# Expert weights in two steps of 1792 columns on one core of a Trainium2

## What is computed

```python
logits = (t @ router).astype(jnp.float32)
top_v, top_i = lax.top_k(logits, TOP_K)                  # TOP_K = 2 of 8
w = jax.nn.softmax(top_v, axis=-1)
combine = jnp.sum(jax.nn.one_hot(top_i, N_EXPERTS) * w[..., None], axis=1)
for e in range(N_EXPERTS):
    out = out + combine[:, e:e + 1] * swiglu(t, w_gate[e], w_up[e], w_down[e])
# swiglu(h, g, u, d) = (silu(h @ g) * (h @ u)) @ d;  g, u: 1024 x 3584, d: 3584 x 1024
```

## Time and profile before

| | us |
|---|---|
| median of 3 runs (1370.97 to 1372.62) | 1371.16 |
| span of the profiled execution, first to last instruction | 1370.1 |
| PE busy | 1328.3 (97%) |
| DVE busy | 735.9 (54%) |
| ACT busy | 630.0 (46%) |
| HBM read | 432.69 MB, 317 GB/s over the span |

### The profile page before, as it was taken

One profiled execution on the slowest core, in us unless ns is written; L12 is line 12 of the kernel. 1 busy time (PEld: TensorE's weight loads), 2 busy tenths in 40 slices (PEclk: granted clock), 3 DMA queues, 4 the chain that ended last, 5 costly groups with the idle time before them and its releaser, 6 DMA issues.

```text
span 1370.1 us, 16033 instructions
## 1 busy us (share of the span) xinstructions
PE 1328.3 (97%) x6410; PEld 936.1 (68%) x6410; DVE 735.9 (54%) x628; ACT 630.0 (46%) x573; POOL 29.0 (2%) x34
## 2 busy tenths in 40 slices
PE   7999999999999999999999999999999999999998
PEld 7978888888888875655665565665665656665665
DVE  6975444445653475454455455454645455455455
ACT  5855334444445463443453434444344444353442
POOL 2000000000310000000000000000000000000000
PEclk9999999999999999999999999999999999999999
DMA  9456556554542349999999999999999999999995
GB/s 333 164 184 216 188 192 193 193 186 128 181 153 92 132 165 361 413 414 414 400 415 409 399 413 413 408 410 409 404 408 412 406 412 410 410 404 413 411 402 225
DMA packets 127881, 434.79 MB, mean 317 GB/s; under 512 B 6960, under 2 KB 9120, under 8 KB 113472
## 3 DMA queue, kind: packets, MB, share of 16 engines
q1 hardware_dynamic: 127344, 433.11, 82.7%
q0 software_dynamic: 368, 0.63, 0.2%
q10 hardware_dynamic: 96, 0.03, 0.0%
HBM read 432.69 MB, written 1.05 MB: 317 GB/s over the span
## 4 chain that ended last, share of the span: by engine, by line
PE 74%; DMA 14%; ACT 4%; DVE 4%; issue 3%; SPq 1%; DVEq 0%; POOL 0%; POOLq 0%; ACTq 0%
PE ps L1381 16%; PE ps L1367 9%; PE ps L909 8%; PE ps L911 8%; PE ps L910 8%; PE ps L1368 8%; PE ps L1369 8%; DMA ring<-in_moe_w_gate_dram 8%; DMA ring<-in_moe_w_up_dram 4%; DVE lows L1533 2%; DMA ring<-in_moe_w_down_dram 2%; ACT whi L548 2%; PE ps L1312 1%; PE ps L1139 1%; SPq L455 1%
## 5 line engine op out<-in xcount | busy, mean ns | idle before, releaser
L1533 DVE TENSOR_TENSOR lows<-ring,whi 128x2048 fp32r<-128x2048 f32 x168 | 382.8, 2290 | 248.1 <-ACT whi L548 248.0
L548 ACT ACTIVATE whi<-ring 128x2048 fp32r<-128x2048 f32 x168 | 320.0, 1912 | 319.3 <-DMA ring<-in_moe_w_up_dram 113.6
L1381 PE MATMUL ps<-ring,xl 128*64 128x512 f32 (+1 forms) x1024 | 204.1, 544 | 4.9 <-DVE xl L2020 3.3
L1526 DVE TENSOR_TENSOR wlo<-raw,whi 128x2048 fp32r<-128x2048 f32 x73 | 166.5, 2288 | 73.5 <-PE ps L911 71.4
L1367 PE MATMUL ps<-whi,hT_hi 128*128 128x512 f32 x448 | 181.2, 405 | 13.0 <-DVE lows L1533 12.8
L541 ACT ACTIVATE whi<-raw 128x2048 fp32r<-128x2048 f32 x73 | 139.5, 1917 | 84.5 <-PE ps L911 82.9
L1368 PE MATMUL ps<-lows,hT_hi 128*128 128x512 f32 x448 | 175.0, 391 | 0.0
L1369 PE MATMUL ps<-whi,hT_lo 128*128 128x512 f32 x448 | 174.5, 390 | 0.0
L909 PE MATMUL ps<-whi,hT_hi 128*128 128x512 f32 x384 | 153.3, 399 | 2.4 <-DVE wlo L1526 1.4
L911 PE MATMUL ps<-whi,hT_lo 128*128 128x512 f32 x384 | 149.7, 390 | 0.0
L910 PE MATMUL ps<-wlo,hT_hi 128*128 128x512 f32 x384 | 149.5, 389 | 0.0
(11 more groups left out here) (307 smaller groups left out, 1314.6 us busy)
## 6 DMA issues: line engine op xcount, KB each, us to landing
ring<-in_moe_w_gate_dram SPq DMA_DIRECT2D x112, 1024.0 KB, 11.9
ring<-in_moe_w_up_dram SPq DMA_DIRECT2D x112, 1024.0 KB, 13.1
ring<-in_moe_w_down_dram SPq DMA_DIRECT2D x112, 1024.0 KB, 13.8
raw<-in_fox_w_in_dram SPq DMA_DIRECT2D x16, 1024.0 KB, 5.3
raw<-in_ffn_w_gate_dram SPq DMA_DIRECT2D x14, 1024.0 KB, 5.1
raw<-in_ffn_w_up_dram SPq DMA_DIRECT2D x14, 1024.0 KB, 5.1
raw<-in_ffn_w_down_dram SPq DMA_DIRECT2D x14, 1024.0 KB, 5.1
raw<-in_lru_w_in_dram SPq DMA_DIRECT2D x8, 1024.0 KB, 11.6
```

Of the source, the lines that this page charges most:

```text
L548: nc.scalar.activation(whi[:, 1 + q % SPLIT], ring[:, slot(i)], ACT.Copy).then_inc(hi_done, 1)
L1381: ins = mm(ps[g * HD:(g + 1) * HD, bank, 0:half], src(k), ring[:, slot(i), cols], start=first and k == 0, stop=last and k == tiles - 1, sk ...
L1526: nc.vector.tensor_tensor(wlo[:, m % LR], raw[:, m % RR], whi[:, m % HR].bitcast(F32), ALU.subtract).then_inc(lo_done, 1)
L1533: nc.vector.tensor_tensor(lows[:, slot(i)], ring[:, slot(i)], whi[:, 1 + q % SPLIT].bitcast(F32), ALU.subtract).then_inc(lo_done, 1)
```

## The change

The class `Group`, the two tables and the code of all five engines that handles the experts are rewritten; the two layers before them stay.

- The 3584 columns are cut in two steps of `W` = 1792. A gate or up unit is one row tile of 1792 columns, 0.9 MB, one run of 7 KB in each partition; a step has 8 of gate, 8 of up and 7 of down for each expert, and a pair has 92 units instead of 84. Names: G0, U0, D0 are the first step's stages, G1, U1, D1 the second's.
- A heavy gate or up unit is 12 matmuls of 448 columns over four banks (4 to 7), and gate, up and the heavy y (banks 4 and 5) use the same banks one after the other. A light unit is 4 calls of 448 columns; the two halves of the array take the even and the odd columns, so that they are read at a step of two.
- y leaves PSUM at the end of each step: `first_y` (ACT) writes the weighted sums of D0 to `yh` and `yl`, `second_y` (DVE) adds those of D1. They are fp32, and so is `ST`; the scatter is one fp32 matmul where it was two fp32r ones.
- D1 of a pair stands behind G0 of the next. A pair's order is G0, D1 of the pair before, U0, G1, D0, U1. After the last pair D1 stands alone (`TAIL`).
- Gathers come in four parts of 8 matmuls, and transposes of the heavy activations in parts of 8 and 6.

```diff
-PAIRS = 4
-PAIR_W = [2 * CW, 2 * CW, 2 * CW, CW]
-PAIR_U = [w // CW * 2 for w in PAIR_W]
+W = F // 2
+CB = W // 4
+TALL, DEEP = KT, W // (2 * P)
+RING, SPLIT = 10, 3
+SKIPS = (6, 25, 36, 47, 58, 69, 80, 90)
+
+
+def wide_turns(kind):
+
+    for b in range(0, TALL, 2):
+        for job in (0, 1):
+            for n in (b, b + 1):
+                yield job, kind, n
+
+
+def down_turns(kind):
+
+    for job, n in ((0, 0), (0, 1), (1, 0), (0, 2), (0, 3), (1, 1), (0, 4), (0, 5), (1, 2), (1, 3), (0, 6), (1, 4),
+                   (1, 5), (1, 6)):
+        yield job, kind, n
...
+REST = [*wide_turns("G1"), *down_turns("D0"), *wide_turns("U1")]
+TAIL = [*down_turns("D1")]
+BODY = [*wide_turns("G0"), *TAIL, *wide_turns("U0"), *REST]
...
+                    src = (moe_w_gate if kind[0] == "G" else moe_w_up)[0][expert, n * P:(n + 1) * P, col:col + W]
+                    sp.dma_start(ring[:, slot(pos), 0:W], src.rearrange("o p c -> p (o c)")
+                                 ).then_inc(arrived[slot(pos)], 16)
...
             pair_loads(Group(loops, 2))
+            pair_loads(Group(loops, 3, TAIL))
...
+            def first_y(group, job):
+
+                if job == 0 and group is not OPENING:
+                    act.wait_ge(m_scat[0], group.nth(0))
+                    act.wait_ge(m_scat[1], group.nth(0))
+                act.wait_ge(used, group.done(job, "D0"))
+                src, dst = (flat(HB, D), yh[:]) if job == 0 else (ps[:, LB], yl[:])
+                nc.scalar.activation(dst, src, ACT.Copy, scale=weight[:, job:job + 1]).then_inc(m_yw, 1)
...
-                for q, y in enumerate((y_hi[job], y_lo[job])):
-                    ins = mm(ps[:, bank], ST[rows, job, t * P:(t + 1) * P], y[rows, cols], start=job == 0 and q == 0,
-                             stop=job == 1 and q == 1)
-                return ins
+                return mm(ps[:, bank], ST[rows, job, t * P:(t + 1) * P], (yh, yl)[job][rows, cols], start=job == 0,
+                          stop=job == 1)
...
+            def wide_unit(group, job, kind, n):
+
+                pos = group.place[job, kind, n]
+                first, last = n == 0, n == TALL - 1
+                if job == 0:
+                    w_hi, w_lo = heavy_halves(group, pos)
+                    for b in range(4):
+                        dst, cols = ps[:, HB + b, 0:CB], slice(b * CB, (b + 1) * CB)
+                        mm(dst, xg_hi[:, n], w_hi[:, cols], start=first, stop=False)
+                        mm(dst, xg_hi[:, n], w_lo[:, cols], start=False, stop=False)
+                        ins = mm(dst, xg_lo[:, n], w_hi[:, cols], start=False, stop=last)
+                else:
+                    pe.wait_ge(arrived[slot(pos)], group.landed(pos))
+                    columns = ring[:, slot(pos), 0:W].rearrange("p (c g) -> p g c", g=2)
+                    for b in range(2):
+                        for g in range(2):
+                            ins = mm(ps[g * HD:(g + 1) * HD, LB + b, 0:CB], xl[:, n],
+                                     columns[:, g, b * CB:(b + 1) * CB], start=first, stop=last, skip_group_check=True)
                 ins.then_inc(used, 1)
...
+                for job, kind, n in wide_turns("U0"):
+                    if n == 0:
+                        pe.wait_ge(m_yd, prev.nth(1 + job, 2))
+                    wide_unit(group, job, kind, n)
+                    if (job, n) == (0, 3):
+                        pe.wait_ge(m_ST, prev.nth(1))
+                        scatter(0)
+                    if (job, n) == (0, 5):
+                        pe.wait_ge(m_acc, prev.nth(1, 2))
+                        scatter(1)
+                    if (job, n) == (0, 7):
+                        pe.wait_ge(m_acc, prev.nth(2, 2))
+                        pe.wait_ge(m_S, group.nth(1))
+                        pe.wait_ge(m_col, group.nth(1))
+                        selection_transposes(group)
...
+            nxt[0] = 0
+            lo_to(0, tail)
+            product(last, 1)
+            lo_to(1, tail)
+            act_T_lo(last, 1, 0)
+            act_T_lo(last, 1, 1, HB + 2)
+            light_product(last, 1)
+            lo_to(DEEP - 1, tail)
```

More of the change, by code:

```diff
@@ L180, in freed, with landed, split, done @@
-def freed(group, q):
-    return (HEAVY[q - SPLIT] - PAIR_UNITS if q < SPLIT else group.heavy[q - SPLIT]) + 1
+    def landed(self, pos):
+        s = slot(pos)
+        return at(16 * (LANDED[pos] - UNLED[s] + self.ahead * PER_SLOT[s]), 16 * PER_SLOT[s], self.i)
+    def split(self, q):
+        return at(N_MOE - HEAVY_LEAD + self.ahead * HEAVY_UNITS + q, HEAVY_UNITS, self.i)
+    def done(self, job, kind):
+        return self.units(max(pos for (j, k, _), pos in self.place.items() if (j, k) == (job, kind)) + 1)
@@ L185, in last_dense, with freed @@
+    def freed(self, q):
+        if self.table is OPEN and q < HEAVY_LEAD + SPLIT:
+            return N_MOE
+        p = max(p for p in range(q - 2 * SPLIT, q) if half_place(p) == half_place(q))
+        return self.units((self.heavy[p] if p in self.heavy else HEAVY_BODY[p + HEAVY_UNITS] - PAIR_UNITS) + 1)
 def last_dense(place):
@@ new lines, in pair_loads @@
+            def pair_loads(group):
+                experts = {}
+                if group is OPENING:
+                    experts["0", 0] = slice(FIRST, FIRST + 1)
+                for pos, (job, kind, n) in enumerate(group.table, group.first):
+                    if group is OPENING and pos in AHEAD:
+                        continue
+                    whose = "D1" if kind == "D1" else "0"
+                    if (whose, job) not in experts:
+                        experts[whose, job] = expert_of(group.before() if kind == "D1" else group, job)
+                    if group is not OPENING or last_in_slot(pos) >= LEAD:
+                        sp.wait_ge(used, group.units(last_in_slot(pos) + 1))
+                    load(group, pos, experts[whose, job])
@@ L817, in light_silu, with rows_view @@
[L817 to L824 removed]
+            def rows_view(bank, ks):
+                return ps[:, bank:bank + ks // 2].rearrange("p b n -> p (b n)").rearrange("p (k c) -> p k c", c=2 * P)
@@ L1372, in light_unit @@
-            def light_unit(group, i, src, bank, first, last):
-                width = group.table[i][4]
-                tiles = UK * CW // width
-                half = width // 2
-                pe.wait_ge(arrived[slot(i)], group.landed(i))
-                for k in range(tiles):
-                    for g in range(2):
-                        cols = slice(k * width + g * half, k * width + (g + 1) * half)
-                        ins = mm(ps[g * HD:(g + 1) * HD, bank, 0:half], src(k), ring[:, slot(i), cols],
-                                 start=first and k == 0, stop=last and k == tiles - 1, skip_group_check=True)
-                ins.then_inc(used, 1)
```

786 lines of the change are left out of this document (408 added, 378 removed).

## The result

The changed kernel takes **1389.3 us**, the kernel before 1371.9 in the same comparison: a ratio of 1.0117, 95% interval [1.0099, 1.0134]. The forecast was 1371, the range ended at 1387, so the kernel is slower by 18 us than forecast and lies outside. The profiled execution spans 1388.2 us.

A forecast was written before the change was run, and what follows sets the result against it. The bound was to move from DMA to PE: 210.3 + 0.6 + 0.7 + 2.6 = 214.2 us a pair against the stream's 211.3. Waits removed would pay for added work: 1371 us (own range 1366 to 1376), full range 1361 to 1387.

The forecast's parts named there:

- The step that failed: Expert pairs: PE's 214.2 us exceeds the stream's 211.3, so PE sets the period; the ring shouldn't run dry.
- The opening: Start of the experts' part: some 2 us of PE idle time stay, with expert weights on DVE between two heavy units' splits.
- Rows of 7 KB: Weight stream: longer rows land at 420 GB/s, 211.3 us a pair with gaps, a gain of 4.7 us a pair.
- Heavy matmuls of 448: Heavy units on PE: 0.200 us a matmul, 384 replacing 336 at 0.227, +0.6 us a pair.
- Light: Light units on PE: 1.56 us each, 32 units 50.0 us a pair, the same as the 28 before; no change.
- the rival on strided reads: Light gates and ups reading every second column cost about 6 us a pair, 1395; sign: starts over 0.40 us apart; chance 0.07.
- Scatter: Full fp32 scatter on PE: 3.84 us each instead of 2.52, +2.6 us a pair, bounds nothing to +3.4.
- Alternations, ACT and DVE, banks: Expert changes cost 0.22 us each, 24 for 21, +0.7 a pair; splits keep their bytes; silu and product waits on shared banks fit.
- the rival on the banks: At stage changes PE waits for product (1.1 us) or silu (0.3), 2.8 us a pair: 1382; chance 0.13.
- PE's base of 210.3: PE's busy time a pair in the kernel before, 210.3 us, to which the change's PE terms were added.
- Tail: Last down stage: PE idles 3.7 us before the light transposes, as the light product stands on DVE behind split and aT halves.
- the case that rows of 7 KB gain nothing: Stream stays at 410 GB/s, 214.7 us a pair: 1377; sign: DMA ahead of ACT in a steady pair's waits; chance 0.06.

The follow-up runs named there:

- the prices granted: Changed kernel with heavy matmuls cut 512+512+512+256, light reads contiguous and cut 512+384 (8 KB down rows kept), and the tail's light product first on DVE: 1381.8 us.
- the better tail: Changed kernel with DVE taking the tail's light product ahead of the two halves of aT instead of behind them: 1386.2 us, ratio 1.0092.
- all third products gone: Changed kernel without the third product (xg_lo by w_hi in gate and up) in every heavy expert unit, gate, up and down: 1362.2 us, ratio 0.9929.
- the shallow ring: Changed kernel with 18 skipped ring slots a pair instead of 8, so transfers run 8.3 units ahead on average instead of 9.2: 1402.0 us, ratio 1.0224.
- its third products left out: Kernel before the change, with the third product left out of every heavy unit of the experts: 1366.0 us, ratio 0.9955.

## Why the prediction was wrong

**The step that failed** is the one from stages to period: "214.2 us a pair, above the stream's 211.3", the period being the larger of two sums, and with it "the ring holds 10 units, some 20 us of work, against 2.2 to land ... It shouldn't run dry". The stage's own arithmetic stood there (PE 32.6 bare, DMA 35.0, "two scatters alone 7.7") and was not followed to the end. A unit takes not 2.2 but about 10 us to land, since others are in flight with it (medians 7.8 to 9.8 us), so of the 20 us little lead is left; what it carried from stage to stage is 4.8 us a pair (223.2 - 218.4), an estimate from the stages above. U0 with 41.5 us by the forecast's own prices (32.6, 7.7 for the scatters and 1.2 for the transposes of the selection) and 175 for the rest make 216.5, not 214.2. With the forecast's prices of gate and up matmuls granted, the kernel still takes 1381.8 with the better tail, some 1385 without. Of the 18 us about 14 are left. Some 2 of them are the scatter's price (4 x 0.54) and 1.5 a fall of the granted clock in the opening (0.69 over 5 us). Most of the rest is PE's idle time, 14.7 us with the better tail, where the forecast had 8.7 (6.3 by the same tail). In the changed kernel itself it doesn't show (8.5 us), because the dearer matmuls fill it.

- *Where they lie*, with the prices granted. A steady pair takes 217.0 us against 215.2 with the idle microsecond allowed, 1.8 more; PE idles 2.0 in it. The opening was taken as PE's with 2 us of idle time and has 7.8 up to the first scatter. There the stream falls behind while PE is slow, 51 to 370 GB/s between 506 and 536, and can't make it up. 4.7 us of the 7.8 are one wait for the light silu, which stands on ACT behind the split of a unit that was 10.13 us on its way (in the changed kernel 3.2 and 8.85 us). The first scatter comes at 767.8 with the prices granted, 768.3 without, and 761.8 with all third products gone. How the rest divides wasn't isolated. The transfer in the chain into that wait:

```profile
542.51 10.13 DMA ring<-in_moe_w_up_dram
```

- *Rows of 7 KB*: right. Forecast 4.7 us a pair, measured 3.9; 420 GB/s as worked out; 212.2 with the gaps against 211.3. (The 1.1% that the prediction works out for 4 KB to 8 KB from 96 bytes a packet is 1.2%; the argument stays.)
- *Heavy matmuls of 448*: mis-sized. 0.2066 for 0.200, +3.1 a pair for +0.6. A straight line through 256 and 512 columns didn't hold.
- *Light*: mis-sized. 1.65 us a unit for 1.56, 32 units +2.8 a pair. Of the 0.09, 0.07 are the step of two; the rival on strided reads (chance 0.07, 6 us a pair) had the mechanism and 2.7 times the size (2.2 us a pair), and its sign came true: calls start 0.41 us apart, over 0.40. By the Trainium skill (SBUF — State Buffer, "Door 1: The DMA port swizzle") the step is free; 3.30 against 3.16 us doesn't agree with it. The prices of heavy and light matmuls together made about 4 of the 18 us, since only what stands in U0, or the sum, counts.
- *Scatter*: 4.11 for 3.84; the bounds held. The term was the dearest of the change (in fp32r it gave back 18 us, 1389.3 to 1371.1), for a reason not seen: it stands in the one stage that can't hide it.
- *Alternations, ACT and DVE, banks*: right. 2 heavy and 2 light units take 24 x 0.2066 + 3.30 = 8.26 of 8.45 us, 0.19 a change; PE waits 0.3 us in all for gt's product before heavy matmuls, so the rival on the banks did not come true. It named 1382, a time nearer than the forecast, by the wrong mechanism: that is luck. With the prices granted its wait does appear, at 0.4 us a pair.
- *PE's base of 210.3* was too high by some 2 us: repriced, the terms give 210.3 + 3.1 + 2.8 + 0.7 + 3.2 = 220.1 and the trace 217.9. (At 0.19 a change, 24 changes cost no more than 21 at 0.22, so 0.7 of the 2 may be that term.) That each of the short waits of the earlier trace rows hides a matmul's modelled end, which counts as busy, would explain the rest; it is not shown.
- *Tail*: right, 3.5 us for 3.7, and in its cause.
- *The direction of the range*: the upper end took in single mishaps, each with its own wait. PE waiting for the stream stood only in the case that rows of 7 KB gain nothing (1377), which did not come true, though its sign did: a transfer ahead of ACT in the chain of a steady pair, which is there at 963.59.

## What to carry to other kernels

Where two engines are within a few per cent of each other, compare them stage by stage and not pair by pair: work that a buffer can't lend across stages costs the sum of the larger times. The lead of a ring is its depth less the time from a freed slot to usable data under load, to be read from the median landing time and not from the bytes of one transfer. Before a saving is taken, ask in which stage it stands: 13 us of PE a pair gave 16 us of the whole launch in the stages beside a full ring and 1 elsewhere. And a sum whose idle term comes out right is no proof that the bound was right: here dearer matmuls filled the time in which PE would have waited.

## What was not expected of the hardware

- fp32r matmuls start 0.227 us apart at 512 columns, 0.2066 at 448 and 0.12 at 256: 448 costs 3% over the line between the others. Why was not tried.
- An fp32 moving operand read at a step of two elements costs 4% (3.30 against 3.16 us for 8 calls); fp32 light calls show no price for the width of 448.
- PE's granted clock fell behind two waits of 3 us that the kernel before doesn't have. The row of the opening, right behind PE's 3.16 us wait for the light silu, and the tail's, around the 3.5 us wait:

```profile
555.00:560.00 5.00, 4.83 (x18) 1.59 (x20) 4.63 (x3) 3.40 (x3) 0.00 (x0) 0.66 0.95 340
```

```profile
1335.00:1350.00 15.00, 11.00 (x53) 8.04 (x50) 10.05 (x7) 6.79 (x6) 0.00 (x0) 0.89 0.97 397
```

  0.66 over 5 us and 0.89 over 15 cost 1.7 us each, time that the engine partly spends at 1.2 instead of 2.4 GHz. With the tail's order changed the wait is 1.3 us and the same stretch runs at full clock, so there the wait cost its own length and, by these rows, half as much again (2.2 us of wait and 1.7 of clock; 3.1 of the 3.9 were measured in the time):

```profile
1335.00:1350.00 15.00, 13.04 (x68) 8.19 (x65) 12.58 (x8) 9.24 (x7) 0.00 (x0) 1.00 1.01 420
```

  In the kernel with the shallow ring the wait of 2.3 us before U0 was enough: the granted clock was 0.86 and 0.80 in the next two stretches of 5 us, and heavy matmuls started 0.37 us apart instead of 0.21 from 979.7 to 983.1.

  A third fall, 0.50 from 495 to 500, stands in the changed kernel's profile ahead of the experts. In that of the kernel with y in fp32r the same stretch is at 1.00, and in that of the kernel before with its third products left out it is at 0.50, so the change is not its cause.
